# Sample attention on a ten-slot beat with four value pages a visit, and sample value rows spread by GpSimd instead of TensorE

## What is computed

```python
xn = rms_norm(x, norm_w)
aq, ak, av, az, mq, mk, mv, mo, mz, ga, gm, mi, mf = split(xn @ w_in)
# attention, 8 heads of 128: the prompt attends to itself; each sample attends to
# 8 cached pages of 128 keys (the 3 best of 4 blocks of 2 pages) and its own key
gate = einsum('bqhd,bnhd->bhqn', qf, k_mean); _, sel = top_k(gate, 3)
s    = einsum('bhqd,bhqkd->bhqk', qf, cache_k[selected pages]) * scale
out  = softmax([s, s_new]) @ [cache_v[selected pages], v_new]
# mLSTM, 4 heads of 256: a matrix state C (256 x 256) for each head and sample
c_new = a_prev * c_prev + einsum('bhs,bhsd,bhse->bhde', a_s, k, v)   # for a sample: one outer product
n_new = a_prev * n_prev + einsum('bhs,bhsd->bhd', a_s, k)
# merge
y = x + (sigmoid(ga) * ((attn * silu(az)) @ w_proj_attn)
       + sigmoid(gm) * ((rms_norm(h * sigmoid(mo)) * silu(mz)) @ w_proj_mlstm)) @ w_out
```

## Time and profile before

| | |
|---|---|
| median of three runs | 469.26 us |
| span of the profiled execution, first to last instruction | 467.2 us |
| TensorE matmul busy | 456.2 us, 98% |
| VectorE busy | 394.1 us, 84% |
| ScalarE busy | 294.4 us, 63% |
| GpSimd busy | 100.9 us, 22% |
| granted TensorE clock | full in every one of the 40 slices |
| moved by DMA | 150.91 MB, mean 323 GB/s |

### The profile page before, as it was taken

The page is one execution under the profiler, slowest core; times in us unless marked ns, Lnnn a source line. Parts: engine busy times, 40 slices in busy tenths (PEclk is TensorE's granted clock), DMA queues, the critical chain, the costliest instruction groups (busy, mean ns, idle before and its releaser), DMA issues.

```text
span 467.2 us, 11345 instructions
## 1 busy us (share of the span) xinstructions
PE 456.2 (98%) x3855; PEld 413.8 (89%) x3855; DVE 394.1 (84%) x1610; ACT 294.4 (63%) x490; POOL 100.9 (22%) x181
## 2 busy tenths in 40 slices
PE   6999999999999999999999999999999999999997
PEld 4899899897879888888899889899898898899997
DVE  3898899699999799999899999799999774668861
ACT  4966545686984496995486695666948357324430
POOL 2040421013323213423321332321223110000000
PEclk9999999999999999999999999999999999999999
DMA  8899699749999999999999999998999985457511
GB/s 304 322 353 407 183 322 371 240 158 340 317 416 408 404 368 354 412 410 408 408 380 315 409 412 409 411 372 303 382 415 409 410 334 188 149 180 261 182 48 48
DMA packets 44858, 150.91 MB, mean 323 GB/s; under 512 B 6192, under 2 KB 7796, under 8 KB 44672
## 3 DMA queue, kind: packets, MB, share of 16 engines
q1 hardware_dynamic: 20368, 70.77, 40.8%
q0 software_dynamic: 19008, 67.20, 37.3%
q10 hardware_dynamic: 5424, 12.21, 6.8%
HBM read 137.37 MB, written 12.76 MB: 321 GB/s over the span
## 4 chain that ended last, share of the span: by engine, by line
PE 70%; ACT 10%; DVE 10%; DMA 4%; issue 4%; ACTq 1%; POOLq 0%; SPq 0%; POOL 0%; DVEq 0%
PE pj L534 28%; PE pj L537 13%; PE wk L534 6%; PE pa L717 4%; PE wk L537 3%; DMA kpages<-in_cache_k 3%; DVE kpages L1170 3%; DVE wlo L1071 2%; ACT L838 2%; ACT whi L818 2%; PE wk L487 2%; DVE cslot L1252 2%; PE wk L639 2%; PE wk L673 1%; DMA cst<-in_consts 1%
## 5 line engine op out<-in xcount | busy, mean ns | idle before, releaser
L534 PE MATMUL pj<-xn,whi 128*128 128x264 f32 x1328 | 180.8, 288 | 1.6 <-ACT mqT L976 1.3
L534 PEld LDWEIGHTS pj<-xn,whi 128*128 128x128 f32 x1328 | 168.4, 189 | 10.2 <-issue 6.2
L1071 DVE TENSOR_TENSOR wlo<-wraw,whi 128x1024 fp32r<-128x1024 f32 x112 | 136.1, 1220 | 8.8 <-ACT whi L818 8.3
L818 ACT ACTIVATE whi<-wraw 128x1024 fp32r<-128x1024 f32 x112 | 117.9, 1053 | 23.1 <-PE wk L537 12.9
L1170 DVE CUSTOM_DVE_ANT_0 kpages<-kpages,qbc 128x128 f32<-128x128 f32 x512 | 115.5, 292 | 5.3 <-DMA kpages<-in_cache_k 5.1
L537 PE MATMUL pj<-xn,wlo 128*128 128x264 f32 x664 | 93.8, 284 | 0.4 <-DVE wlo L1071 0.4
L537 PEld LDWEIGHTS pj<-xn,wlo 128*128 128x128 f32 x664 | 85.5, 188 | 0.6 <-DVE wlo L1071 0.6
L404 POOL DMA_DIRECT2D kpages<-in_cache_k x64 | 34.3, 536 | 165.9 <-DVE sco L1170 141.9
L404 POOL DMA_DIRECT2D vpages<-in_cache_v x64 | 33.9, 530 | 57.9 <-issue 38.9
L1170 DVE DVE_READ_ACCUMULATOR2_ANT sco<- 128x1 f32 x512 | 42.8, 84 | 0.0
L717 PE MATMUL pa<-vpages,prob 128*32 128x256 f32 x512 | 34.2, 385 | 1.7 <-ACT prob L876 1.7
(11 more groups left out here) (271 smaller groups left out, 615.0 us busy)
## 6 DMA issues: line engine op xcount, KB each, us to landing
wraw<-in_weights SPq DMA_DIRECT2D x112, 512.0 KB, 6.8
kpages<-in_cache_k POOLq DMA_DIRECT2D x64, 512.0 KB, 8.1
vpages<-in_cache_v POOLq DMA_DIRECT2D x64, 512.0 KB, 10.8
cslot<-in_states SPq DMA_DIRECT2D x16, 512.0 KB, 9.4
out_C_s<-cslot ACTq DMA_DIRECT2D x16, 512.0 KB, 8.1
xres<-in_tokens SPq DMA_DIRECT2D x1, 1056.0 KB, 5.5
out_k_p<-kT ACTq DMA_DIRECT2D x4, 256.0 KB, 10.2
out_v_p<-v_nat ACTq DMA_DIRECT2D x4, 256.0 KB, 4.7
```

The costliest lines, as they stand in the source:

```text
L534: mm(bank[:, 0:T], whi[:, q, k, :], src[:, g, k, :], start=(k == 0 and g == 0), stop=False)
L818: A(whi[:, n % WSPLIT], wraw[:, n % WRAW], ACT.Copy).then_inc(whi_ready, 1)
L1071: V.tensor_tensor(wlo[:, n % WRAW], wraw[:, n % WRAW], whi[:, n % WSPLIT], ALU.subtract).then_inc(wlo_ready, 1)
```

## The change

It has three parts. The cached samples start every ten slots instead of nine (`STARTS`, `LAGS`); the last sample, which now starts at slot 72, has shorter lags after its last key page. The value pages are taken four a visit, two visits a sample (`VISITS`); their loads are no longer tied to the visits but to slots (`LOADS`). The sample value rows are spread by GpSimd: the product pads are gone, a padded copy `vpad` of the value columns is transposed by four full products instead of two narrow ones, ScalarE copies the result (`mvq`), GpSimd spreads two rows at a time (512 elements) into `mvb`, and `new_states` reads from there. Some steps move: the new normaliser products (line 652) into bank `wk[1]` at i = 8 with a copy on VectorE, `token_scores` from tail slot 12 to 18, its exponential from 14 to 19, `sample_totals` from 18 to 20. GpSimd now waits for each of its broadcasts and reductions to end.

```diff
-START, PERIOD = 2, 9
-SUMS, SELECT, SHIFT, EXP, VALUES, TOTAL, GATHER = 9, 10, 11, 12, 13, 14, 20
+STARTS = [2 + 10 * b for b in range(NB)]
+SUMS, SELECT, SHIFT, EXP, TOTAL, GATHER = range(6)
+LAGS = [(9, 10, 11, 12, 14, 20)] * (NB - 1) + [(8, 9, 10, 10, 11, 13)]
+VISITS = [(13, 17)] * (NB - 2) + [(13, 14), (11, 12)]
+VISIT = PAGES // 2
+LOADS = [[14 + p for p in range(PAGES)]] * (NB - 2) + [[14 + p // 2 for p in range(PAGES)]]
...
+def value_loads(g):
+    return [(b + 1) * PAGES + p for b in range(NB - 1) for p in range(PAGES) if g == STARTS[b] + LOADS[b][p]]
...
+        mvq = sb("mvq", [P, 2 * MHD])
+        vpad = sb("vpad", [P, EC, P + VC // 2])
+        mvb = sb("mvb", [P, 2, 2 * T])
...
@@ gpsimd
+            def spread_values(j, c):
+                pool.wait_ge(mv_ready, 2 * j + 2)
+                if c >= 2:
+                    pool.wait_ge(c_ready, NB * j + 2 * (c - 1))
+                elif j:
+                    pool.wait_ge(c_ready, NB * (j - 1) + 2 * (c + 3))
+                nc.gpsimd.partition_broadcast(mvb[:, c % 2, 0:2 * MHD], mvq[c * VC:c * VC + 1, :]).then_inc(v_spread, 1)
+                pool.wait_ge(v_spread, VG * j + c + 1)
...
-                pair = value_pair(g)
-                if pair is not None:
-                    for s in range(pair[0] * PAGES + 2 * pair[1] + VSLOTS, pair[0] * PAGES + 2 * pair[1] + VSLOTS + 2):
-                        if s < NB * PAGES:
-                            values(s)
+                for s in value_loads(g):
+                    values(s)
+                if g < BODY and g % CHUNKS == 10:
+                    spread_values(g // CHUNKS, 0)
+                    spread_values(g // CHUNKS, 1)
+                if g < BODY and g % CHUNKS in (12, 13):
+                    spread_values(g // CHUNKS, g % CHUNKS - 10)
@@ tensor
                 if i == 9:
                     pe.wait_ge(sw_ready, j + 1)
-                    for n in range(2):
-                        last = tr(wk[3][0:NB, n * P:(n + 1) * P], rawT[:, n, SEQ:T], P)
+                    for pick in range(2):
+                        for n in range(2):
+                            c = pick * MHD + n * P
+                            last = tr(wk[3][:, c:c + P], vpad[:, n, pick * VC // 2:pick * VC // 2 + P], P)
                     last.then_inc(mvtr_ps, 1)
...
-                if i in (11, 12, 13, 14):
-                    pair = i - 11
-                    bank = (wk[0], wk[3], wk[0], wk[2])[pair]
...
-                    for n in range(2):
-                        last = mm(bank[:, n * MHD:(n + 1) * MHD], eye2[:, 2 * pair + n:2 * pair + n + 1].broadcast_to([P, P]),
-                                  mvs2[:, :], start=True, stop=True)
-                    last.then_inc(vbc_ps, 1)
...
-                    for pg in (2 * pair[1], 2 * pair[1] + 1):
+                    for pg in range(VISIT * visit[1], VISIT * (visit[1] + 1)):
@@ scalar
                 if i == 10:
+                    act.wait_ge(mvtr_ps, 2 * j + 2)
+                    act.wait_ge(v_spread, VG * j)
+                    A(mvq[:, :], wk[3][:, :], ACT.Copy).then_inc(mv_ready, 1)
...
-                    A(mvs, wk[3][0:NB, 0:MHD], ACT.Copy)
-                    A(mvs2[0:NB, :], wk[3][0:NB, 0:MHD], ACT.Copy).then_inc(mv_ready, 1)
-                    A(nnew[:, j, :], wk[3][:, MHD:MHD + MHD // VG], ACT.Copy).then_inc(n_ready, 1)
...
+                    if i in (6, 7):
+                        A(vpad[:, i - 6, ds(0, NB, step=VC // 2)], pj[n % 2][:, SEQ:T], ACT.Copy)
@@ vector
-                    dve.wait_ge(vbc_ps, 4 * j + b // 2 + 1)
-                    row = (wk[0], wk[3], wk[0], wk[2])[b // 2][:, b % 2 * MHD:(b % 2 + 1) * MHD]
+                    dve.wait_ge(v_spread, VG * j + b // 2 + 1)
+                    row = mvb[:, b // 2 % 2, b % 2 * MHD:(b % 2 + 1) * MHD]
...
+                    V.tensor_copy(nnew[:, j, :], wk[1][:, NNEW:NNEW + MHD // VG]).then_inc(n_ready, 1)
...
-                if i == 10:
-                    dve.wait_ge(mv_ready, 2 * j + 2)
-                    V.tensor_tensor(mvs2[LO:LO + NB, :], mvs, mvs2[0:NB, :], ALU.subtract).then_inc(mvlo_ready, 1)
```

More of the change, by code:

```diff
@@ L77, with due, value_visit @@
 VC = 32
+NNEW = MHD + VC
 BODY = JOBS * CHUNKS
 LAST = BODY + 5 * KC
-START, PERIOD = 2, 9
-SUMS, SELECT, SHIFT, EXP, VALUES, TOTAL, GATHER = 9, 10, 11, 12, 13, 14, 20
-def due(g, lag):
-    b, left = divmod(g - START - lag, PERIOD)
-    return b if left == 0 and 0 <= b < NB else None
-def key_page(g):
[L97 to L106, removed]
-    return None
+STARTS = [2 + 10 * b for b in range(NB)]
[4 more added lines that the diff above has]
+LOADS = [[14 + p for p in range(PAGES)]] * (NB - 2) + [[14 + p // 2 for p in range(PAGES)]]
+def due(g, step):
+    for b in range(NB):
+        if g == STARTS[b] + LAGS[b][step]:
+            return b
+    return None
+def key_page(g):
+    for b in range(NB):
+        if STARTS[b] <= g < STARTS[b] + PAGES:
+            return b * PAGES + g - STARTS[b]
+    return None
+def value_visit(g):
+    for b in range(NB):
+        for p, lag in enumerate(VISITS[b]):
+            if g == STARTS[b] + lag:
+                return b, p
+    return None
+def value_loads(g):
+    return [(b + 1) * PAGES + p for b in range(NB - 1) for p in range(PAGES) if g == STARTS[b] + LOADS[b][p]]
 class Chain:
@@ L640, in states_side @@
                                    start=(half == 0 and d == 0), stop=(half == 1 and d == EC - 1))
-                    mm(wk[1][:, MHD:MHD + 2 * NB], ones, qsum[:, :, :], start=True, stop=True).then_inc(qc_ps, 1)
-                if i == 9:
-                    pe.wait_ge(sw_ready, j + 1)
-                    for n in range(2):
-                        last = tr(wk[3][0:NB, n * P:(n + 1) * P], rawT[:, n, SEQ:T], P)
-                    last.then_inc(mvtr_ps, 1)
+                    pe.wait_ge(w_ready, j + 1)
                     part = MHD // VG
@@ L651, in states_side @@
                         for q in range(VG):
-                            last = mm(wk[3][q * VC:(q + 1) * VC, MHD:MHD + part], wt[:, col:col + 1].broadcast_to([P, VC]),
+                            last = mm(wk[1][q * VC:(q + 1) * VC, NNEW:NNEW + part], wt[:, col:col + 1].broadcast_to([P, VC]),
                                       mk_nat[:, t, q * part:(q + 1) * part], start=(t == 0), stop=(t == 1))
                     last.then_inc(n_ps, 1)
+                    mm(wk[1][:, MHD:MHD + 2 * NB], ones, qsum[:, :, :], start=True, stop=True).then_inc(qc_ps, 1)
+                if i == 9:
+                    pe.wait_ge(sw_ready, j + 1)
+                    for pick in range(2):
+                        for n in range(2):
+                            c = pick * MHD + n * P
+                            last = tr(wk[3][:, c:c + P], vpad[:, n, pick * VC // 2:pick * VC // 2 + P], P)
+                    last.then_inc(mvtr_ps, 1)
                 if i == 10:
@@ L675, in states_side @@
                     last.then_inc(cn_ps, 1)
[L676 to L691 removed]
                 if i == 14:
[L693 removed]
+                    pe.wait_ge(hst_read, j + 1)
                     pe.wait_ge(sqh_ready, j + 1)
@@ L776, in _ @@
                 elif i == 3:
-                    pe.wait_ge(c_ready, NB * JOBS)
+                    pe.wait_ge(cn_ready, JOBS)
+                    pe.wait_ge(pT_ready, 2 * JOBS)
                 else:
```

47 lines of the change are left out of this document (20 added, 27 removed).

## The result

The changed kernel took 473.26 us (median of 471.5, 473.43, 473.52 and 473.09), the kernel before 469.42 us on the same chip. The ratio is 1.0073, 95% interval 1.0053 to 1.0094: slower by 3.4 us at the ratio, where 463.1 us was forecast. The profiled run of the kernel before has a granted clock of TensorE of 1.000 over the span, and its later runs have 0.999 or 1.000. The runs of the changed kernel have 0.992 (the profiled one, 471.5 us, span 469.8) and 0.989 (the three others).

What follows compares the result with a forecast made beforehand. TensorE's own list was taken as the bound: 4.0 (value rows) + 4.0 (merging) - 0.9 (transposes) = 7.1 us, less 1.0 of waits = 6.1; 469.3 - 6.1 = 463.1 us. Range 459.7 to 467.8 us, its own 461 to 465.

Steps and rivals of the forecast that it cites:

- TensorE's list: TensorE's own sequence of instructions, taken to set the end of the kernel; forecast 7.1 us shorter.
- Value rows less transposes: On TensorE: 32 value-row products in 16 pairs go, saving 4.0 us; added full transposes cost 0.9 us.
- Merging: On TensorE: 32 visits of 16 instructions become 16 of 32, saving 0.25 us each, 4.0 us in all.
- I charge 1 us of new waits: In the body: VectorE's room shrinks by about 2 us, unevenly over a job's slots, costing 1 us.
- Zero cost, at most 2.7 us: In the tail: six more key pages cost nothing, at most 2.7 us if the last sample's sum is late.
- the rival at 475 us: In the tail: key pages land late, 11.8 us lost minus 6.1 gained, slower at 475 us; chance 0.09.
- VectorE becomes the bound: In the body: broadcasts hold VectorE their whole length, TensorE waits for wlo; 466.3, up to 468 us; chance 0.18.
- the charge: On VectorE: outer products reading SBUF beside sixteen new broadcasts lose 0.47 us each, 7.5 us; bounds 0 to 12.8 us.
- Merging saves nothing: On TensorE: each page costs its 1.20 us wherever it stands; gain only 2.1 us, 467.2 us; chance 0.09.
- Everything pays: On TensorE: pairs count 5.9 us and no wait is added; gain 9.3 us, 460.0 us; chance 0.14.
- Launch and end: Outside the profiled span: the median is 2.1 us above the span, and the change leaves this as it is.

Runs made afterwards that it cites:

- the repaired version: Changed kernel with sample 6's value pages requested two slots earlier, next job's rows on ScalarE's DMA queue, `sample_tokens` at tail slot 8: 463.15 us, ratio 0.9868.

## Why the prediction was wrong, point by point

**What held.** TensorE's list got shorter as forecast: 8.0 us (forecast 7.1). A merged visit takes 1.86 us, "about 1.9" was forecast. With the three waits gone the time is 463.15 us, where 463.1 had been forecast for the change as it was.

**Two terms of the list were mis-sized against each other.** Value rows less transposes: 3.1 forecast, 2.0 to 2.2 measured. The products alone, from start to start, gave back 5.2 us; the added transposes took 0.6 of it, and 2.6 went to the instructions beside them. Merging: 4.0 forecast, bound 4.3; 5.8 to 6.0 measured for the whole schedule (450.2 against 456.2, 448.2 against 454.0), about 5 for the merging alone. The visits' own starts give 32 x 1.00 - 16 x 1.86 = 2.2 us of it. The rest is spread thin: added up from start to start, the wlo products give 0.9 us and no other group of small work more than 0.7. I also put 12 of the 16 merged visits in the body; samples 0 to 4 have ten. The sum doesn't use that number.

**The failed step is the price of waits.** It had three parts.
- "I charge 1 us of new waits" (body). TensorE's idle time grew by 7.1 us. I looked for new waits in the balance of busy times: VectorE is busy 183.9 us in 100 to 300, less than before. The wait came from a single row at one job border, asked for and landed at nearly the same time as before while the slots had moved 2.9 us ahead and the two key pages that had covered it were gone. VectorE stood still 3.88 us although it had room on average.
- The tail: "Zero cost, at most 2.7 us". I had added the traffic of a stretch at 411 GB/s, but did not walk the eight value loads of sample 6 through their slots. The last is asked for in slot 73 and used in slot 76, and needs 12.5 us. Rows of before had a price near that, 13.85 us for a key page; I applied it to key pages (the rival at 475 us) and not to value pages, whose loads the change had untied from the visits. `sample_tokens` at slot 67, which the diff doesn't touch, was not asked at all: 1.9 us.
- The clock was in no case. Two pauses of 2.6 and 3.2 us cost 3.5 us more in the profiled execution. Without it the profiled run would have been 469.8 - 3.5 = 466.3 us of span against 467.2, hardly faster; with it, it was slower. The three other executions, at 0.989, lose some 0.003 x 470 = 1.4 us more.

**The rivals.** "VectorE becomes the bound" fell for the change itself: 463.15 us with nothing taken from VectorE. VectorE was charged 7.5 us for the broadcasts. With the rests gone (2.0 us) and the new copies (0.9 us) set off, they cost it 2.5 + 2.0 - 0.9 = 3.6 us in the repaired version and 5.4 + 2.0 - 0.9 = 6.5 us on nine slots (estimates from busy times of 395.5 and 398.0, 394.1 and 399.5 us), so the charge was too high but of the right order. The place was wrong: I laid it on the outer products, which lost 0.8 us, and most of it fell on the products of key pages. In the repaired version TensorE saw next to none of it. "Merging saves nothing" fell. "Everything pays" overshot the list (9.3 against 8.0) and has no waits. The slower rival had the sign and the stretch, late pages in the tail, but the wrong tiles: TensorE waited for value pages there. VectorE's waits for key pages are 5.7 us in the whole run, 5.1 before.

**Launch and end.** "Which the change leaves": 2.1 us before, 471.5 - 469.8 = 1.7 us after. No part of the miss.

**The range** left out everything above 467.8 us but for the rival of 0.09. With a value page priced at the 13.85 us of the earlier trace rows against three slots of 2.92 us, a wait of 13.85 - 8.76 = 5.1 us was in reach, and 463.1 + 5.1 = 468.2 us already lay outside.

## What to carry to other kernels

When loads are tied to slots instead of to the use before them, walk each one from its request to its first use at the landing time of that stretch, also for tiles that the change doesn't seem to touch. Busy shares don't show a wait for one small row, nor that a result of an engine that works in order stands behind another wait of it. If an engine stands at the end of the path, price a pause of TensorE by more than its length, and after such a change look at the granted clock first: a dip points to the stall to mend.

## What the runs showed of the hardware

One pause of 3.0 us in an otherwise unchanged kernel cost 5.3 us by the medians (2.5 to 5.8), with the granted clock at 0.69 over the next 5 us; one of 1.3 us cost 0.7 us at a clock of 1.00. Pauses of 2.6 and 3.2 us were followed by 0.70 and 0.66, one of 2.05 us on nine slots by 0.81. One of 3.4 us was followed by 0.50: 5 x (0.16 + 0.50 + 0.02) = 3.4 us lost from 195 to 210, twice the 1.7 us of the pause put in. In the version with three repairs no pause in body and tail is longer than 1.54 us and the clock stays full. The wait of 1.87 us in slot 67 had no dip behind it either. The Trainium skill (TensorE: Matmul & The Clock Gate, Terms) puts the penalty at the time on the lower level times one less the granted share. By it the mean clock of 0.992 in the changed kernel stands for a loss of 0.008 x 470 = 3.8 us (an estimate). The account above left 3.5 us: the trace agrees.

A full-width broadcast of 512 elements shows as 1.12 us on average, one of 8 elements still as 0.62 us: more than half of the operation's time is not in its width.
